# Low parts of the weight chunks on GpSimd: four quarters spread over a step, or one run of four at a step's end

## The reference, cut to what matters

```python
proj = h @ w_in                                   # 1024 inputs, 4040 output columns
score = sum_h w_idx[h] * relu(q_idx[h] @ k_idx.T)  # 8 heads, every query against every key
top_val, top_idx = lax.top_k(score, 256)           # the 256 best keys of each query
```

## Time and profile before

| | us |
|---|---|
| three runs | 3702.49, 3703.35, 3707.95 |
| the profiled execution, its own time | 3713.29 |
| its span, first to last instruction | 3711.0 |
| TensorE busy in the span | 3479.2 (94%) |
| VectorE busy | 2222.7 (60%) |
| ScalarE busy | 1925.1 (52%) |
| GpSimd busy | 1701.6 (46%) |

### The profile page before, as it was taken

One profiled execution on the slowest core, in us unless ns is written; L12 is line 12 of the kernel. 1 busy time (PEld: TensorE's weight loads), 2 busy tenths in 40 slices (PEclk: granted clock), 3 DMA queues, 4 the chain that ended last, 5 costly groups with the idle time before them and its releaser, 6 DMA issues. The chain is left out here.

```text
span 3711.0 us, 52572 instructions
## 1 busy us (share of the span) xinstructions
PE 3479.2 (94%) x17924; PEld 2900.8 (78%) x17924; DVE 2222.7 (60%) x3097; ACT 1925.1 (52%) x3592; POOL 1701.6 (46%) x1806
## 2 busy tenths in 40 slices
PE   6988998898989999999997998999999999999997
PEld 5776777777767888988996777778887888888786
DVE  5236888787632565676533666764546545565867
ACT  3223787788635798887553332343334333344443
POOL 5342344765311322222004665556664665554756
PEclk9999999999989999999998999999999999999998
DMA  8344324332221111100005445654445444365663
GB/s 272 130 132 113 98 83 133 113 92 79 79 74 44 40 42 35 35 20 16 23 11 187 165 169 177 227 199 149 168 141 195 153 142 151 129 246 190 236 227 132
DMA packets 338458, 468.44 MB, mean 126 GB/s; under 512 B 23184, under 2 KB 225120, under 8 KB 334992
## 3 DMA queue, kind: packets, MB, share of 16 engines
q1 hardware_dynamic: 310064, 387.47, 32.1%
q10 hardware_dynamic: 28128, 77.60, 5.7%
HBM read 311.21 MB, written 153.78 MB: 125 GB/s over the span
## 5 line engine op out<-in xcount | busy, mean ns | idle before, releaser
L2629 POOL TENSOR_TENSOR ff_rounded_ring<-ff_raw,ff_rounded_ring 128x512 fp32r<-128x512 f32 x264 | 383.1, 1462 | 294.8 <-ACT ff_rounded_ring L2776 292.1
L100 PE MATMUL ff_bank<-ff_rounded_pair,ff_rounded_ring 128*128 128x512 f32 x1232 | 484.3, 393 | 17.7 <-POOL ff_rounded_ring L2629 12.8
L101 PE MATMUL ff_bank<-ff_rounded_pair,ff_rounded_ring 128*128 128x512 f32 x1232 | 482.9, 392 | 0.0
L102 PE MATMUL ff_bank<-ff_rounded_pair,ff_rounded_ring 128*128 128x512 f32 x1232 | 482.5, 392 | 0.0
L1796 PE MATMUL at_ctx<-at_p_t,at_c_nat 128*128 128x128 f32 (+1 forms) x2432 | 344.1, 282 | 8.1 <-ACT at_ctx_t L1912 7.3
L1796 PEld LDWEIGHTS at_ctx<-at_p_t,at_c_nat 128*128 128x128 f32 (+1 forms) x2432 | 300.7, 191 | 35.4 <-ACT at_ctx_t L1912 13.0
L1906 ACT ACTIVATE at_p_t<-at_turn 128x512 f32<-128x512 f32 (+4 forms) x416 | 213.1, 544 | 206.8 <-PE at_turn L1773 176.8
L2634 POOL TENSOR_TENSOR ff_rounded_ring<-ff_raw,ff_rounded_ring 128x512 fp32r<-128x512 f32 x154 | 212.2, 1383 | 174.6 <-ACT ff_rounded_ring L2826 174.6
L3057 DVE TENSOR_TENSOR ff_rounded_a_ring<-ff_f_q,ff_rounded_a_ring 128x512 fp32r<-128x512 f32 x154 | 210.1, 1374 | 130.8 <-ACT ff_rounded_a_ring L2818 129.7
L100 PEld LDWEIGHTS ff_bank<-ff_rounded_pair,ff_rounded_ring 128*128 128x128 f32 x1232 | 233.5, 190 | 69.8 <-POOL ff_rounded_ring L2629 14.8
L102 PEld LDWEIGHTS ff_bank<-ff_rounded_pair,ff_rounded_ring 128*128 128x128 f32 x1232 | 233.5, 190 | 48.8
(11 more groups left out here) (389 smaller groups left out, 9078.6 us busy)
## 6 DMA issues: line engine op xcount, KB each, us to landing
f_kept<-ff_resid SPq DMA_DIRECT2D x154, 256.0 KB, 2.4
ff_f_q<-f_kept ACTq DMA_DIRECT2D x12, 2816.0 KB, 11.0
pj_raw<-in_w_in SPq DMA_DIRECT2D x58, 512.0 KB, 4.5
proj<-se_row SPq DMA_DIRECT2D x104, 256.0 KB, 2.6
ff_raw<-in_w_ff_gate SPq DMA_DIRECT2D x22, 1024.0 KB, 10.8
ff_raw<-in_w_ff_up SPq DMA_DIRECT2D x22, 1024.0 KB, 6.2
ff_raw<-down_comb SPq DMA_DIRECT2D x88, 256.0 KB, 2.7
ff_raw<-in_w_ff_down SPq DMA_DIRECT2D x66, 256.0 KB, 3.0
```

What stands on the lines that cost most here:

```text
L100: pe.matmul(out, lhs_lo, rhs_hi, start=start, stop=False, skip_group_check=goes_on)
L101: pe.matmul(out, lhs_hi, rhs_hi, start=False, stop=False, skip_group_check=goes_on)
L102: return pe.matmul(out, lhs_hi, rhs_lo, start=False, stop=stop, skip_group_check=goes_on)
L2629: pool.tensor_tensor(ring[:, step % RING, 1, :].rearrange("p (k c) -> p k c", c=P), f_operand(it, q, m), f32(ring[:, step % RING, 0, :]).r ...
```

## The change

The quarters behind the judgements go; a chunk's low part is made in one run of four quarters at the end of GpSimd's step s+1, behind both judgements of half 1 and ahead of `low_index`. The table `SOON` and `low_parts_soon` go with them, since all chunks are now treated as those two were. The four instructions, their sizes, their one wait (for the high part) and their one signal stay as they are; no DMA and no instruction of another engine is moved.

```diff
-SOON = (FIRST_HALF - 2, FIRST_HALF - 1)
...
-                    def low_parts(n, quarters):
+                    def low_parts(n):
                         for u in units_in(n):
                             k = UNITS[u][2]
-                            if u == LAST_OF_LOAD[k] and k + 2 < len(LOADS) and u not in SOON:
-                                low_part(k + 2, quarters)
-
-                    def low_parts_soon(n):
-                        for u in units_in(n):
-                            if u in SOON:
-                                low_part(UNITS[u][2] + 2)
+                            if u == LAST_OF_LOAD[k] and k + 2 < len(LOADS):
+                                low_part(k + 2)
...
                     for n in range(FIRST_STEP, LAST_STEP + 1):
                         m = n + IDX_AHEAD
                         if n <= -IDX_AHEAD:
-                            low_parts(n - 2, range(4))
+                            low_parts(n - 2)
+                        if n == -IDX_AHEAD:
+                            low_parts(n - 1)
                         for u in units_behind(n, 1):
                             if u < NK:
                                 inverse_root(u)
                         if n <= -IDX_AHEAD:
                             continue
                         part_a(n, 0)
-                        low_parts(n - 2, [0])
                         part_b(n, 0)
-                        low_parts(n - 2, [1])
                         part_a(n, 1)
-                        low_parts(n - 2, [2])
                         part_b(n, 1)
-                        low_parts(n - 2, [3])
-                        low_parts_soon(n - 1)
+                        low_parts(n - 1)
                         if m >= 0 and m % HEADS == 4 and m // HEADS + 1 < TILES:
                             low_index(m // HEADS + 1)
```

## The result

The changed kernel takes 3737.47 us (median of six runs, 3735.03 to 3745.93) against 3704.6 us for the kernel before (six runs, 3699.65 to 3708.72): a ratio of 1.009, 95% interval 1.0076 to 1.0103, or 28 to 38 us more. The forecast was 3726.7 with a range up to 3737, so the direction held and the size was some 10 us short, 0.5 us outside the range. The profiled execution has a span of 3744.1 us against 3711.0.

A forecast was written before the change was run, and what follows sets the result against it. From 620 to 865 us a loop of VectorE tally and GpSimd judgement was taken to bind, then ScalarE, then TensorE. 17.4 + 3.6 + 2.2 + 1 - 0.9 = +23.3 us on 3703.35 gave 3726.7 us, range 3713 to 3737.

The forecast's parts named there:

- 44, 52, 60, 68: run, then index: In these steps the next judgement stands behind both the run of four and `low_index`: +17.4 us.
- runs where only A is judged: Steps 46, 54, 56, 58, 62 and 70: a run of four outlasts its cover, +6.5 us, less 1.4 in step 70.
- both judged, what the run costs: Steps 48, 50, 64 and 66: the run behind B's judgement delays the next tally, 9.7 us in all.
- both judged, what goes: Near the chunks of steps 48, 50, 64 and 66, waits caused by the old quarters go: 7.5 us.
- B's last judgement: Steps 48 and 64: old quarters no longer stand in front of B's last judgement, on which VectorE waits: -1.5 us.
- start: Step -32: the root moves behind a run, 3.5 us late, mostly taken up later; +1, bounds -1 and +3.5.
- step 81: TensorE, by then the bound, is spared a wait of 0.93 us: -0.9 us.
- Ahead of 620 us VectorE judges A itself, so GpSimd is hardly in the loop: Stretch ahead of 620 us: GpSimd hardly matters to the loop; forecast 0 for steps 0 to 44.
- The runs stay out of the way: Rival: high parts come before the judgement and quarters keep their 0.74 us; +3, or 3706 us; chance 0.20.
- Judgements without quarters between them: Rival, faster: GpSimd has the judgements to itself, -9.0 with -0.9 at step 81; 3693.4 us; chance 0.07.
- TensorE is the bound after all: Rival, faster still: TensorE's 28.7 us of waits for low parts come back; 3674.7 us; chance 0.03.
- The signs: TensorE's low-part waits under 5 us; VectorE's candidate waits up some 20, mainly four of 3 to 6 at `low_index` steps.

The follow-up runs named there:

- the sign alone: Kernel before, with the chunk whose quarters stand in step 8 made in a run at the end of step 7, ahead of search A's sign; ratio 1.0018.
- The root alone: Kernel before, with the run of four of step -31 put ahead of the inverse root of step -32; block +2.3 us, ratio 1.0019.
- small quarters: Kernel before, with each quarter of chunks 34 to 49 cut to 128x16 elements, the rest left out; -10.1 us from step 44 to 80, ratio 0.9963.
- four pieces: Kernel before, with the low half of the query index made in four pieces in steps 44 and 60; block -0.8 us, ratio 1.000.

## Why the prediction was right and wrong

| step of the prediction | forecast, us | measured, us |
|---|---|---|
| 44, 52, 60, 68: run, then index | +17.4 | waits before the tallies of 45, 53, 61, 69 +8.3, +5.4, +3.9, +5.4 = +23.0; the four joins -5.1: +17.9 |
| runs where only A is judged | +6.5, less 1.4 in 70 | 47, 55, 63, 71: +1.4 each, 57 and 59: +0.46 each = +6.6 |
| both judged, what the run costs | +9.7 | 49, 51, 65, 67: +2.8, +2.6, +2.8, +2.6 = +10.8 |
| both judged, what goes | -7.5 | -7.3 |
| B's last judgement | -1.5 | -0.8 |
| start | +1 | +2.3 alone, +4.7 in the changed kernel |
| steps 0 to 44 | 0 | +6.8; the sign alone +4.2 |
| step 81 | -0.9 | -1.2 |

The block is 33.2 us longer where 23.3 was forecast. Of the 9.9 us missing, 3.7 lie in the start, 6.8 in steps 0 to 44, and the rest is 0.6 the other way.

- **The loop of steps 44 to 72 was read rightly**, from rows of the kernel before alone: 23.2 forecast, 22.9 measured. That the two agree within 0.3 us is partly luck. The waits before tallies grew by 32.0 us; some 9 of that are not in the time, since the joins got shorter (5.1 us), and VectorE's waits for ScalarE (26.0 to 22.6 us) and in front of the extra tally of B (line 1206; 11.2 to 9.8) shrank, of which the forecast had only the 2.9 us that it took off steps 68 and 70. The four steps with the index came as 6.9, 3.9, 2.9 and 4.2 us (the new wait less what the join gave back), where 5.8, 4.4, 4.0 and 3.2 were forecast.
- **The join was misread, without harm.** The prediction said that no row shows whether a join and a GpSimd operation get in each other's way. Its own group did: the join of 2.14 us in the earlier trace rows lasts so long because the index runs beside it; by itself it takes 0.70. The rule of the Trainium skill that it weighed (SBUF — State Buffer, Who interferes with whom) holds for the join as well, by these numbers. It did no harm because a shorter join (5.1 us in the four steps) only lets VectorE wait longer for the same candidate: 23.0 us of new waits less 5.1 is 17.9, where 17.4 was forecast.
- **The step that failed first** is "most of it taken up by the waits of the following steps; I put +1". The root alone costs 2.3 us, which stay to the end; the delay of the one tile of keys goes to all that follow. The upper bound, +3.5, would have held the root alone, not the 4.7 us by which the changed kernel starts late, whose other half is open.
- **The step that failed most** is "Ahead of 620 us VectorE judges A itself, so GpSimd is hardly in the loop". GpSimd still makes the sign of each search, one short operation in 16 steps on which VectorE waits at once, and the new order puts a run in front of it whose high part comes 10.6 us after GpSimd is free. So steps 0 to 44 stand in the sum at nothing and cost 6.8 us, of which the sign alone explains 4.2 in the kernel before and 5.2 in the changed one (6.9 less 1.7, steps 4 to 16). The windows and waits of the stretch ahead of 620 us were never set against GpSimd's new order; a mean over the stretch would not have shown it, the order of the queue at steps 7 and 8 does.
- **The rivals.** "The runs stay out of the way" fell: 3737 against 3706. (Its terms, 5.6 + 2.1 + 4 - 9.0 - 0.9, add to +1.8, not to +3; with the +1 of the start it is +2.8.) "Judgements without quarters between them" was right about the price, 9.0 forecast and 10.1 measured with small quarters, but the runs bring their own. "TensorE is the bound after all" fell clearly: its waits for low parts went from 28.7 to 5.6 us and the kernel became slower, and the runs in steps 41 to 72 alone cut those waits to 9.6 us and cost 22 us. The rule of the Trainium skill (Perfetto Trace Analysis, Optimization Strategies) says to speed up engines that block the critical path to keep the matmul engine going; the prediction gave the rule without its words on the critical path, and they are the ones that count here.
- **The signs.** TensorE's waits fell to 5.6, a little over the 5 given. VectorE's for the candidate grew by 26 us, not some 20. Four waits at the steps with the index came as 8.45, 5.46, 4.03 and 5.46 us, the first above the 3 to 6 given. GpSimd waits for the high part 4.79 us in 44, 1.74 in 52 and 2.04 in 68; in 50 and 64 only 0.2. The waits of 1.3 us in steps 50 to 52 and 66 to 68 are 0.11.

## What to carry to other kernels

A wait of the busiest engine is worth something only if nobody behind it has slack; here the buffers covered TensorE's waits of up to 3.4 us, in one place even 10.5 us, while a loop of two other engines set the pace. When work is moved in an engine's queue, list every instruction behind it on which another engine waits, the rare ones too (a sign in 16 steps, a root per tile), and check for each whether the moved work waits for something itself: a short operation behind a waiting one inherits the whole wait. And do it for all stretches, not only for the one that looks bound.

## What the runs showed of the hardware

- **A VectorE operation with two inputs in SBUF stands still while a GpSimd operation runs, until that one has ended.** Join of 128x912: 0.63 us alone, 2.06 beside the index of 2.39 us, which ended 1.57 us after the join began. It holds the other way too: four quarters take 2.83 us undisturbed (step 44) and 3.46 to 4.08 with an addition or a join beside them (steps 52 and 60), and a quarter of the index 1.10 in place of 0.74 when a join got in first. This is the exclusive lock of which the Trainium skill speaks (SBUF — State Buffer, Who interferes with whom); the trace agrees, by these numbers. So the length of one GpSimd operation is itself a cost, though four pieces won only 0.2 to 0.3 us per step here.
- **How well a trace repeats depends on the stretch.** The kernel before, profiled twice, repeats within 0.3 us in the second block from step 4 on and differs by 11.7 us behind it (2677.9 and 2666.2 us); over all kernels here that untouched code takes between 2660.4 and 2680.7 us. Five kernels with a run in front of the root, one code up to there, differ by 4.2 us at step 0 (0.5 to 4.7). Effects of 2 to 6 us could be read only from the trace, step by step.
